# Down projection of an MLP: 24 of 32 inner blocks in seven products instead of eight, from weights split anew in each slot

## What is computed

```python
pn = _rmsnorm(xp, ln_mlp[l])
xp = xp + jnp.square(jax.nn.relu(pn @ w_up[l])) @ w_down[l]
```

## Time and profile before

| | |
|---|---|
| median of 3 runs | 2366.32 us |
| span of the profiled execution, first to last instruction | 2364.1 us |
| TensorE busy | 2353.3 us, 15933 matmuls |
| VectorE, ScalarE, POOL busy | 933.2, 650.3, 275.9 us |
| MLP in pass 0 | about 434 to 1138 us |
| MLP in pass 1 | about 1595 to 2353 us |

### The profile page before, as it was taken

The page is one execution under the profiler, slowest core; times in us unless marked ns, Lnnn a source line. Parts: engine busy times, 40 slices in busy tenths (PEclk is TensorE's granted clock), DMA queues, the critical chain, the costliest instruction groups (busy, mean ns, idle before and its releaser), DMA issues.

```text
span 2364.1 us, 38969 instructions
## 1 busy us (share of the span) xinstructions
PE 2353.3 (100%) x15933; PEld 2130.4 (90%) x15933; DVE 933.2 (39%) x1610; ACT 650.3 (28%) x1259; POOL 275.9 (12%) x276
## 2 busy tenths in 40 slices
PE   9999999999999999999999999999999999999998
PEld 7878888888888888888999999999999999999998
DVE  8766664421121221223876676533212212211224
ACT  5454543321220220222444434422101101200211
POOL 0000002222222222222000000000000000000000
PEclk9999999999999999999999999999999999999999
DMA  6333336344444444454422222422222222222223
GB/s 230 112 108 108 111 112 225 134 143 151 135 158 135 147 144 150 143 204 146 144 99 90 73 91 72 161 90 90 89 89 90 89 89 89 89 89 89 89 90 128
DMA packets 87989, 284.42 MB, mean 120 GB/s; under 512 B 15936, under 2 KB 19136, under 8 KB 87872
## 3 DMA queue, kind: packets, MB, share of 16 engines
q1 hardware_dynamic: 56880, 171.33, 21.2%
q0 software_dynamic: 27968, 101.72, 13.3%
q10 hardware_dynamic: 3024, 9.67, 1.1%
HBM read 171.07 MB, written 111.62 MB: 120 GB/s over the span
## 4 chain that ended last, share of the span: by engine, by line
PE 98%; DVE 1%; DMA 1%; issue 0%; ACTq 0%; ACT 0%; DVEq 0%
PE bank L615 31%; PE bank L617 31%; PE bank L616 30%; PE aux L809 1%; PE aux L717 1%; PE aux L780 1%; PE aux L750 1%; PE aux L779 1%; DMA xs<-in_xT 1%; DVE xy L1837 0%; PE aux L636 0%; PE aux L723 0%; PE aux L799 0%; PE aux L740 0%; PE aux L691 0%; PE aux L704 0%
## 5 line engine op out<-in xcount | busy, mean ns | idle before, releaser
L615 PE MATMUL bank<-a_hi,w_hi 128*128 128x358 f32 (+3 forms) x2560 | 915.2, 357 | 1.0 <-DVE w_lo L1663 0.4
L617 PE MATMUL bank<-a_hi,w_lo 128*128 128x358 f32 (+3 forms) x2560 | 899.4, 351 | 0.0
L616 PE MATMUL bank<-a_lo,w_hi 128*128 128x358 f32 (+3 forms) x2560 | 898.8, 351 | 0.0
L615 PEld LDWEIGHTS bank<-a_hi,w_hi 128*128 128x128 f32 x2560 | 480.6, 188 | 46.4 <-issue 3.0
L617 PEld LDWEIGHTS bank<-a_hi,w_lo 128*128 128x128 f32 x2560 | 481.4, 188 | 42.0
L616 PEld LDWEIGHTS bank<-a_lo,w_hi 128*128 128x128 f32 x2560 | 481.0, 188 | 42.1 <-issue 1.7
L615 PE MATMUL bank<-b_hi,w_hi 128*128 128x358 f32 (+3 forms) x1280 | 450.2, 352 | 0.0
L616 PE MATMUL bank<-b_lo,w_hi 128*128 128x358 f32 (+3 forms) x1280 | 449.1, 351 | 0.0
L617 PE MATMUL bank<-b_hi,w_lo 128*128 128x358 f32 (+3 forms) x1280 | 449.1, 351 | 0.0
L928 ACT ACTIVATE a_hi<-tmp 128x356 f32 (+5 forms) x160 | 88.3, 552 | 817.3 <-DVE tmp L1780 817.3
L1790 DVE TENSOR_TENSOR xy<-xy,bank 128x356 f32 (+6 forms) x160 | 94.1, 588 | 551.4 <-PE bank L617 551.2
(11 more groups left out here) (192 smaller groups left out, 1417.7 us busy)
## 6 DMA issues: line engine op xcount, KB each, us to landing
w_st<-in_wall SPq DMA_DIRECT2D x96, 512.0 KB, 4.2
kept_hi<-w_hi SPq DMA_DIRECT2D x96, 512.0 KB, 4.9
kept_lo<-w_lo SPq DMA_DIRECT2D x96, 512.0 KB, 5.7
w_hi<-kept_hi POOLq DMA_DIRECT2D x96, 512.0 KB, 3.9
w_lo<-kept_lo POOLq DMA_DIRECT2D x96, 512.0 KB, 4.6
xs<-in_xT ACTq DMA_DIRECT2D x8, 536.0 KB, 7.4
xy<-in_xT SPq DMA_DIRECT2D x8, 536.0 KB, 8.4
xy<-in_xT ACTq DMA_DIRECT2D x8, 512.0 KB, 7.4
```

Source lines behind the costliest of these rows:

```text
L615: pe.matmul(ps, wh, xh, start=(j == 0), stop=False)
L616: pe.matmul(ps, wh, xl, start=False, stop=False)
L617: mm = pe.matmul(ps, wl, xh, start=False, stop=(j == 7))
```

## The change

The MLP's weights are now worked as 6 groups (`SG`) of 4 up blocks and 8 half-filled down slots, and after them a last round of 8 up and 8 down blocks in the form of before. In a group, inner channels are two pairs (`j`) of two blocks, outputs are paired as block m with m + 4 (`PAIRS`), and the first two token tiles form the two columns (504 and 504 in pass 0, 358 and 358 in pass 1). So each pair is a 2 x 2 times 2 x 2 product of blocks, and it is done in seven products (`seven`) instead of eight, in a form with 15 additions. The third tile of pass 1 is done plainly (`third`).

- Weights: the four sums of weight quadrants are made in DRAM (`sums`) by 48 copies and 4 accumulating DMAs, all issued from POOL ahead of its other work. An even slot of a pair holds four quadrants, an odd one three (in pass 1 a fourth for the third tile). Each slot is split as before, by one ScalarE rounding and one POOL subtract of all 1024 columns, and TensorE waits for the whole of it. The slot can be rounded again when its products are done (`consumed`).
- Operands: for each `j`, VectorE and ScalarE form seven operands B11, B21, B22, T1 to T4 from the four squared hidden tiles, each with a rounded part and a rest (`ACT_STEPS`, `DVE_STEPS`; 11 VectorE steps and 4 evacuations for each `j`).
- Results: products use the four `aux` banks as x_, y_, z_, v_. VectorE adds or subtracts them into the quadrants of `xy` with 7 operations (`gather`, `take`); product 5 accumulates on top of product 1's bank after it has been read once, 6 on 3's and 7 on 4's. `xy` is kept in another basis between `to_basis` and `from_basis` (8 operations each).
- Split MLP weights are no longer stored and reloaded: pass 1 loads and splits its MLP blocks again. The MLP's loops are unrolled.

```diff
+SG = 6
+SBLK = 12
+SHID = 4
+PAIRS = 4
+PROD = 7
...
+ACT_STEPS = [["h12", "h11", "hi3", "h22", "hi5", "hi2", "hi1", "h21", "hi6"],
...
+DVE_STEPS = [["lo0", "t3", "lo3", "t2", "lo5", "t1", "lo1", "lo2", "lo4", "t6", "lo6"],
...
+        def consumed(eng, p, n):
+
+            if n < MLP0:
+                eng.wait_ge(unit_done, unit_no(p, n, NT[p] - 1) + 1)
+            elif n >= LAST0:
+                eng.wait_ge(unit_done, last_unit(p, NT[p] * (n - LAST0 + 1)))
+            else:
+                g, k = divmod(n - MLP0, SBLK)
+                if k < SHID:
+                    eng.wait_ge(unit_done, group_unit(p, g, NT[p] * (k + 1)))
+                else:
+                    j, s = divmod(k - SHID, 2)
+                    eng.wait_ge(product_done, product_no(p, g, j) + (PROD if s else 4))
...
+            for n in range(BLOCKS - 2):
+                sync.wait_ge(w_ready, n + 1)
+                load(n + 2)
+                if n < MLP0:
+                    keep(n, n % 2)
...
+            for g in range(SG):
+                r = slice(PAIRS * P * g, PAIRS * P * (g + 1))
+                top, low = down_rows(g, 0), down_rows(g, PAIRS)
+                for i in range(3):
+                    pool.dma_start(first[r, QW * i:QW * (i + 1)], top[:, 0:QW]).then_inc(summed, 16)
...
+            pool.wait_ge(summed, 16 * COPIES)
+            pool.dma_start(first[:, 2 * QW:3 * QW], second[:, 3 * QW:4 * QW], accum_op=ALU.add).then_inc(summed, 16)
+            pool.dma_start(first[:, 3 * QW:4 * QW], second[:, 2 * QW:3 * QW], accum_op=ALU.add).then_inc(summed, 16)
+            pool.wait_ge(summed, 16 * (COPIES + 2))
+            pool.dma_start(first[:, QW:2 * QW], first[:, 3 * QW:4 * QW], accum_op=ALU.add).then_inc(summed, 16)
+            pool.wait_ge(summed, 16 * (COPIES + 3))
+            pool.dma_start(second[:, QW:2 * QW], first[:, QW:2 * QW], accum_op=ALU.add).then_inc(summed, 16)
...
+                def seven(g, j):
...
+                    s0, s1 = n % 2, (n + 1) % 2
+                    weights(p, n)
+                    earlier(5)
+                    product(1, x_, s0, 0, B11, True)
+                    if p:
+                        third(0, s0, 0, 0, True)
+                    product(2, v_, s0, 1, T2, True, True)
+                    earlier(6)
+                    product(3, y_, s0, 2, T3, True)
+                    earlier(7)
+                    product(4, z_, s0, 3, T1, True)
+                    weights(p, n + 1)
+                    pe.wait_ge(product_read, base + 1)
+                    product(5, x_, s1, 0, B21, False, True)
+                    if p:
+                        third(0, s1, 0, 1, False)
+                    pe.wait_ge(product_read, base + 3)
+                    product(6, y_, s1, 1, B22, False, True)
+                    pe.wait_ge(product_read, base + 4)
+                    product(7, z_, s1, 2, T4, False, True)
...
+                    for ub in range(SHID):
+                        round_weights(n0 + ub + 1, p)
+                        for i, t in enumerate(UP_ORDER[p]):
+                            if ub == SHID - 1 and i == nt - 1:
+                                round_weights(n0 + SHID + 1, p)
+                            hidden(g, ub, i, t)
+                    for ub in range(SHID + 2, SBLK + 1):
+                        round_weights(n0 + ub, p)
...
+                    take(1, x22, x_, ALU.subtract)
+                    dve.wait_ge(product_read, base + 1)
+                    take(2, x22, v_, ALU.subtract)
+                    dve.wait_ge(product_read, base + 2)
+                    take(3, x22, y_, ALU.subtract)
+                    dve.wait_ge(product_read, base + 3)
+                    take(4, x22, z_, ALU.subtract)
+                    take(5, x11, x_, ALU.add)
```

More of the change, by code:

```diff
@@ L515, in _ @@
             load_small(0)
[L516 to L525, removed]
+            for n in range(BLOCKS - 2):
+                sync.wait_ge(w_ready, n + 1)
+                load(n + 2)
+                if n < MLP0:
+                    keep(n, n % 2)
+            sync.wait_ge(unit_done, last_unit(0, KB * NT[0]))
             load_small(1)
@@ L870, in _ @@
[L870 to L904, removed]
@@ new lines, in three @@
+                def three(ps, slot, chunk, right, opens, closes, ready=None):
+                    for kb in range(2):
+                        if ready is not None and kb:
+                            pe.wait_ge(h_dve, ready)
+                        c = QW * chunk + P * kb
+                        wh, wl = (w[:, slot, c:c + P] for w in (w_hi, w_lo))
+                        xh, xl = right(kb)
+                        pe.matmul(ps, wh, xh, start=opens and kb == 0, stop=False, skip_group_check=True)
+                        pe.matmul(ps, wh, xl, start=False, stop=False, skip_group_check=True)
+                        mm = pe.matmul(ps, wl, xh, start=False, stop=closes and kb == 1, skip_group_check=True)
+                    return mm
@@ new lines, in _, with add_residual @@
+                for g in range(SG):
+                    for ub in range(SHID):
+                        for i, t in enumerate(UP_ORDER[p]):
+                            hidden(g, ub, i, t)
+                        if g == 0 and ub == 0:
+                            to_basis()
+                    for j in range(PAIRS):
+                        gather(g, j)
+                from_basis()
+                def add_residual(m, t):
+                    c0, w = KEPT[p][t]
+                    u = last_unit(p, KB * nt + FINAL_AT[p][(m, t)])
+                    dve.wait_ge(unit_done, u + 1)
+                    x = xy[:, m, c0:c0 + w]
+                    tt(x, x, bank[u % 4][:, 0:w], ALU.add).then_inc(bank_free[u % 4], 1)
@@ L1803, in last_sum @@
+                dve.wait_ge(h_ready, KB * sum(NT[:p + 1]))
                 def last_sum(m, t):
```

435 lines of the change are left out of this document (320 added, 115 removed).

## The result

The changed kernel takes 2340.38 us (median of 4 runs, 2339.17 to 2341.17) against 2366.31 for the kernel before: a ratio of 0.989 (95% interval 0.9876 to 0.9904). It is faster by 25.9 us, which the ranges of both kernels' runs bear out (they are 24.6 us apart). The time lies in the predicted range of 2308 to 2356, but 16 us above the predicted 2324, and just outside the likeliest case's own range (2310 to 2340). In the profiled execution the span falls from 2364.1 to 2338.3.

What follows compares the result with a forecast made beforehand. TensorE was taken as the bound, busy for all but 11 of 2364 us. Removed matmuls, 56.2 us, less costs of 2, 9, 1 and 2, gave 42.2 us less: a median of 2324 us, range 2308 to 2356.

Steps and rivals of the forecast that it cites:

- the likeliest case: The forecast as told, 2324 us with its own range of 2310 to 2340, given a chance of 0.58.
- Matmuls: MLP down projection: each pass loses 144 matmuls, saving 32.7 us in pass 0 and 23.5 in pass 1, together 56.2.
- The weight slots: Down stages of pass 0: a 3.87 us refill just fits under a 4.08 us odd slot; cost 0 to 7, taken as 2.
- The turn from up to down: Pass 0's six groups: product 5 waits 1.5 us each, as POOL's subtract delays `lo4`; 1 to 10 us, taken as 9.
- The change of basis: First group of pass 0: `to_basis` comes just behind the reciprocals on VectorE; cost 0 to 3 us, taken as 1.
- The rival cause that the text did name: In pass 0, ScalarE's rounding of the next block waits in order behind VectorE's change of basis: 0 to 3 us.
- The start: At the very start, other x loads and constants may come later beside the sums' transfers: 0 to 5 us, taken as 2.
- The sums in time: Sums in DRAM: POOL is free at about 170 to 350 us, before its first subtract at 365.02; taken as in time.
- the rival with a slower sign: Late sums in DRAM hold POOL beyond about 407 us, making the kernel slower than before; chance of slower 0.12.
- rival 2: Sums in DRAM are late, POOL free only after 365 us, each us beyond costing TensorE one; chance 0.19.

Runs made afterwards that it cites:

- The longer refill: Changed kernel, but POOL clears 312 spare columns before its subtract in three even down slots of each pass 0 group: 2342.5 us.
- the short subtract: Changed kernel, but in pass 0 POOL's subtract for each group's first odd slot covers only 512 of 1024 columns: 2334.1 us.
- the takes in front: Changed kernel, but at pass 0's turn VectorE takes products 1 and 2 before B21's rest, and 3 and 4 before T4's rest: 2330.1 us.
- Late sums: Changed kernel, but POOL issues the first copy of the sums only after the fourth weight block is split: 2332.9 us.
- the spread version: Changed kernel, but each pass's first group has two of the eight change-of-basis operations behind each of four hidden units: 2339.1 us.

## Why the prediction came out right in direction and 16 us short

- **Matmuls, 56.2 us.** The count was right (15645 in the page), and pass 1, where nothing stood in the way, gave 22.7 of 23.5. From 1688 to 1780 us TensorE is never idle, with 563 matmuls of 0.1634 us:

```profile
1688.00:1780.00 92.00, 92.00 (x563) 92.00 (x563) 40.14 (x75) 26.54 (x43) 29.48 (x13) 1.00 0.21 69
```

- **The pace, taken as unchanged.** In pass 0 a matmul took 0.2285 instead of 0.2273: 2160 x 0.0012 = 2.6 us that were no term of the sum.
- **The weight slots, 2 us.** The margin was right and the 2 us weren't needed: at the change from odd to even slots in a group there is no gap, and in one group (at 619 us) the next up stage came 0.14 us late. The longer refill shows that the margin was real and about 0.15 us.
- **The turn from up to down, 9 us.** Right in mechanism and size: 9.9 us, at product 5, behind the first take, with `lo4` blocked by POOL (1.96 us). Both halves are shown, by the short subtract and by the takes in front. In pass 1 there is no such wait.
- **The change of basis, 1 us.** Mis-sized: 6.3. The rival cause that the text did name, ScalarE's rounding waiting in order behind VectorE's arrears, was bounded by 3 us. Two things were not in the bound: POOL's subtract also blocks a change-of-basis operation (2.88 us instead of 0.68), and the wait cost TensorE its clock, 13 matmuls at nearly double time (2.7 us). With the 2.6 us of the pace and the 9.9 of the turn, these 6.3 make up the 19 us by which pass 0's MLP is over 665.6.
- **The start, 2 us.** This step failed. It allowed for later x loads and constants, and gave weight loads "some 10 us to spare". The allowance held for the load: block 2's came 10 us later (30.5 instead of 20.6 us), before TensorE wanted it. What was too late was block 0's second store (22.7 us instead of 9.1), on which the rounding of block 2 waits, and which the sum priced nowhere. The stall of 5.0 us plus the lower clock behind it made 7.4 of the 9.1 us. Late sums bring 7.8 of them back in the profile.
- **The sums in time.** Right, and the rival with a slower sign didn't come. POOL issued the first accumulation at 131.7 and the last at 225.9 us, with a median of 31.1 us to landing; it was free at 228 us (forecast: 170 to 350), 145 us before its first subtract. The last one landed at 257.6 us, so the 0.36 ms estimated in rival 2 were too long. The 48 copies took 120 us from first issue to the last one's landing. An estimate from the DMA share against that of the kernel before in the same stretches: the copies took (0.97 - 0.44) x 119 = 63 us of all engines, near the undoubled 71, and the accumulations (0.97 - 0.33) x 126 = 81, between 35 and 106. The sum took POOL's issuing to run on beside the transfers. It did not: two of these rows stand behind no wait of the program:

```profile
30.45 0.64 POOL L706 DMA_DIRECT2D sums<-in_wall  x1
88.65 0.63 POOL L707 DMA_DIRECT2D sums<-in_wall  x1 [57.57 <-issue]
...
131.72 2.41 POOL L709 DMA_DIRECT2D sums<-sums  x1 [32.60 <-DMA sums<-in_wall]
164.66 2.38 POOL L710 DMA_DIRECT2D sums<-sums  x1 [30.54 <-issue]
```

After 31 copies POOL stood until the last of them had landed (88.0 us), and before the second accumulation until the first had (164.4). With the late sums it stood after 31 copies too, from 60.2 to 115.5 us. Issuing itself was priced at 165 us and took POOL 39. The standing cost nothing, since POOL had no other work; with a subtract behind it that TensorE waits for, it could have.

- **Not foreseen at all:** the third stage's 1.5 us, pass 1's loads beside a reload that was on the path.

The two surprises share a form. A transfer or an operation was judged by its own deadline, and not by what stood beside it (the stores of block 0) or behind it in order (ScalarE's rounding).

## What to carry to other kernels

When bulk transfers are put early because nothing needs them soon, look at which transfers of the first blocks they share the engines with, stores that free a buffer included: here 25 MB cost 7.5 us begun at 12 us and nothing that the trace shows begun at 41. And look at what the issuing engine has to do meanwhile: POOL was held for 57.6 us with its copies. When operations are added to an engine, put them where the timeline shows it idle, and look at what other engines' instructions stand in order behind it; moved within the busy stretch, they moved the wait. And where an engine's in-order list has a read that releases a bank behind a subtraction that another engine may block, put the read first: that alone took away six waits, 9.9 us here.

## What the runs showed of the hardware

- TensorE's clock fell to its lower level behind waits of 5.0 and 3.5 us, for 11 and 13 matmuls, and behind a wait of 2.0 us (in the spread version, 19 us after one of 1.2) for 8. It did not behind the single waits of 1.4 us. A stall's price was so up to 1.8 times its length (6.3 for 3.5 us). The number isn't fixed: behind the same wait at 480 us (3.5 to 3.7 us) it was 8, 9, 9, 9, 13, 13 and 14 in seven versions.
- DRAM to DRAM, 48 copies of 512 KB beside the normal traffic landed in 26.6 us each (median), several at once, and an accumulating DMA of 3 MB in 31.1 us. From 12 to 257 us, while they ran, the DMA engines were 97% busy on average.
- POOL issued 31 such copies and then stood, in both placements (57.6 and 55.3 us). In the changed kernel the next copy was issued 0.7 us after the 31st had landed, and the second accumulation 0.3 us after the first had. Why it stands isn't shown.
- A matmul of 496 columns took 0.2237 us in one loop and 0.2252 in the groups of the other, at the full clock in both. Neither width, nor the tile's place, nor unrolling explains it, and it is the same whether VectorE, ScalarE or POOL is busy beside TensorE or idle. The cause stays open.
- A VectorE operation on two SBUF operands that meets POOL's subtract is held until that has ended, as the prediction had it from the earlier trace rows: 0.68 us became 1.96 and 2.88, both ending 0.55 us behind the subtract, and 0.85 when the subtract was half as long. That POOL is held by VectorE isn't shown.
